# Norms applied after the products: weighted residual rows into TensorE, the factor per token into the results

## The chip, the cores and the metric

One NeuronCore of a Trainium2 chip runs the whole program in one launch. The metric is the device time of that execution in microseconds (us); lower is better.

## The reference, cut to what matters

Four decoder layers (mixers a, b, c, a) over 512 prompt tokens and 8 x 8 sample tokens, so 576 tokens of 1024 features, all in float32:

```
x = x + mixer(rmsnorm(x, g_mix));  x = x + convffn(rmsnorm(x, g_ffn))          per layer
rmsnorm(x, g) = x * rsqrt(mean(x*x, over features) + 1e-6) * g
conv_ffn:  u = xn @ w_up;  gate, val = u[:, :2816], u[:, 2816:]
           h = silu(causal_conv3(gate) + conv_b) * val;  return h @ w_down
fox (b):   proj = xn @ w_in  ->  q, k (normed per head of 64), v, g (sigmoid), logf
conv_mix (c): proj = xn @ w_in -> gb, gc, h;  z = causal_conv3(gc * h);  return (gb * z) @ w_out
```

There are eight norms: one ahead of each mixer and one ahead of each conv_ffn. The mixer of layers 0 and 3 (RWKV-7, "a") needs the normed rows themselves, to mix neighbouring tokens; the six other norms feed only matrix products, in which the factor per token, rsqrt(...), can be taken out of the product.

## The kernel before, in words

Activations lie with the features on the partitions: `x` is 8 rows of 128 features by 576 tokens. The weights come from HBM as 415 chunks of 1024 x 128 (512 KB), one after the other through four buffers `raw`. Each chunk is split on the fly into two float32r parts, `wh` on ScalarE (`split_hi`, L358) and `wl` on VectorE (`split_lo`, L365), each with two buffers; the activations are split in the same way into `xh`, `xl` (or `hh`, `hl`). A product is then hi*hi + hi*lo + lo*hi: `chunk_mm` (L368 to L386) runs 8 rows x 2 halves of 288 tokens x 3 matmuls = 48 matmuls for one chunk, into one of two PSUM tiles that alternate. The buffer of a chunk's weights comes free when the chunk is done (`s_mm`), a PSUM tile when its result has been read (`s_ev`). ScalarE, VectorE and TensorE each run their instructions in the order written; semaphores join them. Most phases are hardware loops (`Fori`), those of mixer a and the last down product are written out straight.

Each layer is a chain of phases: the mixer's products, the mixer proper, `out` (8 chunks, `res_*` with one chunk per tile), `up` (44 chunks, gate and value tiles in turn, `up_*`), `down` (24 chunks of 8, 8 and 6 rows, three per tile, `res_*`). In `res_*`, for each finished tile: ScalarE and VectorE first split the weights of the chunk that comes two later, then VectorE adds the tile to the row of `x` (L461), ScalarE squares the new row (L450), and TensorE, one tile later, sums the squares over the features with a matmul against ones (L478; the last row's at L425 in `add_squares`).

Behind the last row of squares stands the norm: ScalarE takes the root (`norm_act`, L410), VectorE the reciprocal (L391), and then for each of the 8 rows VectorE writes `xt` = x * g * rstd (L401), ScalarE copies it to `xh` (L413), and VectorE writes `xl` = xt - xh (L395). The first chunk of the next phase waits for `xl` row by row (`row_ready`, L376).

In `up_*`, ScalarE copies the gate tile out of PSUM (L507, L508) and makes the first tap of the convolution with its bias (L510); VectorE adds two taps (L527, L531); ScalarE applies silu (L514); VectorE multiplies with the value tile in PSUM (L536, L537) and the result is split into `hh` (ScalarE, L517) and `hl` (VectorE, L541). In layer 1, `qk_*` runs the 16 chunks of q and k first (per chunk: copy out of PSUM L1392, square L1397, a head sum on TensorE L1430, root L1384, reciprocal L1411, multiply L1414), in loops of four, with the head sum of each chunk behind the next chunk and the fourth head sum at the end of the iteration (L1439); then come the 16 chunks of v and g, with one copy or sigmoid each (L1368), and one chunk for the forget gate (`forget_*`, L1447 and on), behind which the attention starts.

Of the kernel before, what the change touches and what calls it, by code (L numbers as in the profile page):

```python
# [21 lines left out]
D = 1024  # L22
# [92 lines left out]
def build_program(nc, I, O, mixers=MIXERS):  # L115
# [3 lines left out]
    with ctx:  # L119
# [36 lines left out]
        cs = at("cs", [KF, 2 * NS], F32, f.take(4 * KF * 2 * NS))  # L156
        assert f.at <= nc.sbuf_usable_end, (f.at, nc.sbuf_usable_end)
# [13 lines left out]
        qn, rn = at("qn", [2, T], F32, b.at), at("rn", [2, T], F32, b.at + 8 * T)  # L171
        sc = at("sc", [2, 2, TP], F32, b.take(16 * TP))
# [73 lines left out]
        s_const, s_xin = sem("s_const"), sem("s_xin")  # L246
# [6 lines left out]
        s_sq, s_squ = sem("s_sq"), sem("s_squ")  # L253
        s_pad, s_t0, s_cv1, s_cv = sem("s_pad"), sem("s_t0"), sem("s_cv1"), sem("s_cv")
# [28 lines left out]
        NCONST = 2  # L283
        for layer, (kind, idx) in enumerate(mixers):
            names = []
            if kind == "a":
                names += [("r", 8, 8), ("k", 8, 8), ("v", 8, 8), ("g1", 1, 1), ("w1", 1, 1), ("a1", 1, 1)]
            elif kind == "b":
                names += [("qk", 16, 16), ("vg", 16, 16), ("f", 1, 1)]
            elif kind == "c":  # L290
                names += [("in", 24, 24)]
# [15 lines left out]
        n_norm, row0 = {}, {}  # L307
        q = r0 = 0
        for layer, (kind, _) in enumerate(mixers):
            if kind != "n":  # L310
                n_norm[layer, "mix"], row0[layer, "mix"] = q, r0
                q, r0 = q + 1, r0 + (len(MIX) if kind == "a" else 1) * KD
            n_norm[layer, "ffn"], row0[layer, "ffn"] = q, r0
            q, r0 = q + 1, r0 + KD
# [4 lines left out]
        def squ0(r):  # L319
            return KD + r * (2 + KD)  # L320

# [46 lines left out]
        def chunk_mm(pe, c, n, rh, rl, k0=0, nk=CH, first=True, last=True, i=0, cstep=0, nstep=0, row_ready=None,  # L368
                     row_used=None):
# [4 lines left out]
            for k in range(nk):  # L374
                if row_ready is not None:
# [13 lines left out]
        def norm_dve(dve, q, r0, col):  # L389
            dve.wait_ge(s_rs, q + 1)  # L390
            dve.reciprocal(rstd[:], rstd[:]).then_inc(s_rr, 1)  # L391

            def lo(k):
                dve.wait_ge(s_xh, r0 + k + 1)
                dve.tensor_tensor(xl[:, k], xt[:, k % 2], xh[:, k].bitcast(F32), ALU.subtract).then_inc(s_xl, 1)  # L395

            dve.wait_ge(s_rr, q + 1)
            for k in range(KD):
                if k >= 2:
                    dve.wait_ge(s_xl, r0 + k - 1)  # L400
                dve.scalar_tensor_tensor(xt[:, k % 2], x[:, k], par[:, col + k:col + k + 1], rstd[:],  # L401
                                         ALU.mult, ALU.mult).then_inc(s_xt, 1)
                if k >= 1:
                    lo(k - 1)
            lo(KD - 1)

        def norm_act(act, q, r0):
            act.activation(warm[:], eps[:], ACT.Sqrt)
            act.wait_ge(s_squ, KD + q * (2 + KD))
            act.activation(rstd[:], pst(STAT), ACT.Sqrt, bias=eps[:], scale=1.0 / D).then_inc(s_rs, 1)  # L410
# [18 lines left out]
        def rounds(eng, n, ph):  # L429

            if ph.c0 + ph.nch == NCHUNK:
# [7 lines left out]
        def res_act(act, ph, per):  # L439
# [3 lines left out]
            for i in rounds(act, 2, ph):  # L443
                for j in range(4):
                    for e in range(per):
                        split_hi(act, ph.c0 + per * j + e + 2, i, 4 * per)
                    n = ph.n0 + j
# [3 lines left out]
                        .then_inc(s_sq, 1)  # L451

        def res_dve(dve, ph, per):
            for i in rounds(dve, 2, ph):
                for j in range(4):
                    for e in range(per):
                        split_lo(dve, ph.c0 + per * j + e + 2, i, 4 * per)
# [1832 lines left out]
```

## Time and profile before

| | |
|---|---|
| median of 3 runs | 4210.56 us (4200.27 to 4211.14) |
| the profiled execution | 4210.09 us, span of its trace 4208.2 us |
| TensorE busy | 3826.8 us, 91% of the span |
| VectorE, ScalarE, GpSimd busy | 1793.6, 1512.9, 287.1 us |
| mean granted TensorE clock | 0.944 of full speed |
| read from HBM | 297.30 MB |

Busy time is the sum of an engine's instructions; the span runs from the first to the last instruction. TensorE's clock has two levels here, 2.4 GHz (1.00) and 1.2 GHz (0.50); a mean between them says what share of a stretch ran at which.

### The profile page before, as it was taken

Reading aid. Unit: us, or ns where it says so; the run is one execution under the profiler, and the core shown is the slowest. Engines: PE = TensorE matmul, PEld = TensorE weight load, DVE = VectorE, ACT = ScalarE, POOL = GpSimd, SP = SyncE. Lnnn points to the kernel's source line nnn. Section 1 sums busy time; section 2 is a strip of 40 time slices with the busy share of each in tenths; the row PEclk is TensorE's granted clock in tenths of the full one; section 3 lists DMA queues with packets and bytes.
Section 4 is the critical chain, followed back from the end, with each engine's and each line's share of the span. In section 5 each row is a group of like instructions: output and inputs, shape, how many; then the busy total and the mean of one; then the engine's idle time right before and its main releaser. Section 6 shows DMA issues by size and latency. Waiting matters only on the chain.

```text
span 4208.2 us, 93473 instructions
## 1 busy us (share of the span) xinstructions
PE 3826.8 (91%) x40189; PEld 3504.9 (83%) x40189; DVE 1793.6 (43%) x2245; ACT 1512.9 (36%) x2377; POOL 287.1 (7%) x556
## 2 busy tenths in 40 slices
PE   6968889899998989889998989999796888989999
PEld 5947784799998965589998989999794778489999
DVE  4375543444326434344423334432536554334432
ACT  2344441244323333334422224442233544124431
POOL 0011211000000000000000000000001212000000
PEclk9979996899999999999999999999897999689999
DMA  3200000122221258622222222222220000012222
GB/s 115 76 26 3 3 23 23 47 80 85 82 85 55 75 201 310 226 67 80 84 83 71 85 73 74 81 82 85 74 81 21 3 3 23 23 52 80 84 82 78
DMA packets 95902, 314.16 MB, mean 75 GB/s; under 512 B 18946, under 2 KB 20226, under 8 KB 94866
## 3 DMA queue, kind: packets, MB, share of 16 engines
q1 hardware_dynamic: 87410, 285.25, 20.6%
q10 hardware_dynamic: 8224, 24.88, 1.5%
q8 instruction: 223, 3.65, 0.4%
q14 instruction: 45, 0.37, 0.0%
HBM read 297.30 MB, written 12.79 MB: 74 GB/s over the span
## 4 chain that ended last, share of the span: by engine, by line
PE 56%; DVE 6%; ACT 4%; issue 1%; DMA 0%; ACTq 0%; SPq 0%; DVEq 0%
PE ps L381 14%; PE ps L383 14%; PE ps L382 14%; PE ps L993 3%; PE ps L478 1%; DVE xt L686 1%; PE ps L1237 1%; DVE xl L680 1%; DVE xt L401 1%; PE ps L1569 1%; PE ps L1230 1%; PE ps L1604 1%; PE ps L1624 1%; PE ps L1668 1%; PE ps L802 0%
## 5 line engine op out<-in xcount | busy, mean ns | idle before, releaser
L381 PE MATMUL ps<-xh,wh 128*128 128x288 f32 x4976 | 1504.3, 302 | 122.8 <-DVE xl L680 70.2
L382 PE MATMUL ps<-xl,wh 128*128 128x288 f32 x4976 | 1479.0, 297 | 0.0
L383 PE MATMUL ps<-xh,wl 128*128 128x288 f32 x4976 | 1473.0, 296 | 0.0
L365 DVE TENSOR_TENSOR wl<-raw,wh 128x1024 fp32r<-128x1024 f32 x415 | 508.3, 1225 | 1413.2 <-ACT wh L358 1412.9
L381 PEld LDWEIGHTS ps<-xh,wh 128*128 128x128 f32 x4976 | 943.0, 190 | 149.3 <-issue 97.1
L358 ACT ACTIVATE wh<-raw 128x1024 fp32r<-128x1024 f32 x415 | 440.0, 1061 | 1424.7 <-PE ps L383 1416.8
L382 PEld LDWEIGHTS ps<-xl,wh 128*128 128x128 f32 x4976 | 945.9, 190 | 2.3
L383 PEld LDWEIGHTS ps<-xh,wl 128*128 128x128 f32 x4976 | 947.4, 190 | 0.0
L381 PE MATMUL ps<-hh,wh 128*128 128x288 f32 x1536 | 463.4, 302 | 0.0
L383 PE MATMUL ps<-hh,wl 128*128 128x288 f32 x1536 | 455.4, 297 | 0.0
L382 PE MATMUL ps<-hl,wh 128*128 128x288 f32 x1536 | 448.6, 292 | 0.0
L382 PEld LDWEIGHTS ps<-hl,wh 128*128 128x128 f32 x1536 | 293.2, 191 | 2.1
L381 PEld LDWEIGHTS ps<-hh,wh 128*128 128x128 f32 x1536 | 289.2, 188 | 2.7 <-issue 0.6
L383 PEld LDWEIGHTS ps<-hh,wl 128*128 128x128 f32 x1536 | 288.4, 188 | 0.0
L993 PE MATMUL ps<-m,m 64*64 64x64 f32 x5952 | 228.5, 222 | 27.3 <-DVE m L1022 26.2
L993 PEld LDWEIGHTS ps<-m,m 64*64 64x64 f32 x5952 | 207.1, 139 | 32.2 <-DVE m L1022 28.2
L1022 DVE TENSOR_TENSOR m<-ps,m 128x512 f32<-128x512 f32 x100 | 68.7, 687 | 165.7 <-PE ps L993 165.6
L564 POOL COPY co<-gate 128x2 f32 x96 | 50.1, 522 | 1142.2 <-ACT gate L508 1014.2
L536 DVE TENSOR_TENSOR hf<-conv,ps 128x512 f32<-128x512 f32 x88 | 60.6, 688 | 155.1 <-PE ps L383 155.1
L701 ACT ACTIVATE xh<-xt 128x576 fp32r<-128x576 f32 x96 | 66.0, 687 | 106.8 <-DVE xt L686 106.2
L514 ACT ACTIVATE conv<-conv 128x592 f32<-128x592 f32 x88 | 61.6, 700 | 118.3 <-DVE conv L531 118.3
L1007 ACT ACTIVATE m<-ps 128x512 f32<-128x512 f32 x120 | 71.1, 595 | 81.1 <-PE ps L993 81.1
(300 smaller groups left out, 4565.7 us busy)
## 6 DMA issues: line engine op xcount, KB each, us to landing
raw<-in_w SPq DMA_DIRECT2D x415, 512.0 KB, 3.5
kp<-in_cache_k SPq DMA_DIRECT2D x64, 512.0 KB, 5.6
vp<-in_cache_v SPq DMA_DIRECT2D x64, 512.0 KB, 5.7
rkv<-in_wkv ACTq DMA_DIRECT2D x2, 2048.0 KB, 10.1
out_wkvs<-rkv ACTq DMA_DIRECT2D x2, 2048.0 KB, 7.3
x<-in_x ACTq DMA_DIRECT2D x1, 2304.0 KB, 13.0
out_k<-qk ACTq DMA_DIRECT2D x1, 2304.0 KB, 8.2
out_v<-vg ACTq DMA_DIRECT2D x1, 2304.0 KB, 13.0
```

The lines of the kernel that those rows point to most:

```text
L358: act.activation(wh[:, c % SPL], raw[:, c % RAWS], ACT.Copy).then_inc(s_hi, 1)
L365: dve.tensor_tensor(wl[:, c % SPL], raw[:, c % RAWS], wh[:, c % SPL].bitcast(F32), ALU.subtract).then_inc(s_lo, 1)
L381: pe.matmul(out, w_h, rhs_h, start=(first and k == 0), stop=False)
L382: pe.matmul(out, w_h, rhs_l, start=False, stop=False)
L383: mm = pe.matmul(out, w_l, rhs_h, start=False, stop=(last and k == nk - 1))
L514: act.activation(conv[:, u, 2:GW], conv[:, u, 2:GW], ACT.Silu).then_inc(s_si, 1)
L536: dve.tensor_tensor(tok(hf[:], 0), hist(conv[:, u], 0), tok(pst((n + 1) % 2), 0), ALU.mult)
L564: pool.tensor_copy(co[:, bass.ds(i * 2 + u, 1), 0:2], one(gate[:, u, GS - 2:GS]))
L701: act.activation(xh[:, k], xt[:, k % 2], ACT.Copy).then_inc(s_xh, 1)
L993: mm = pe.matmul(bank(bk)[r, p * CT:(p + 1) * CT], operand(sl, left, p)[r], mview("ist")[r] if right == "ist" else operand(sl, right, p)[r ...
L1007: act.activation(flat(sl[to][:]), bank(bk), ACT.Copy).then_inc(a_e, 1)
L1022: dve.tensor_tensor(sl[to][:], src, sl[by][:], ALU.add).then_inc(a_d, 1)
```

## The change

Six norms (all but the mixer norms of layers 0 and 3) are no longer applied to the rows that enter the products. `xh`, `xl` become the split of x * g, made row by row as soon as a row of `x` is final (`raw_hi`, `raw_lo`). Where the product that ends the row does not read `xh` (`down`, and `out` of layer 2) this stands inside the loop over the tiles; where it does (`out` of layers 0, 1 and 3) rows 0 to 6 are rewritten in place during the last tile, each when TensorE has used it (`s_gu`), and these phases are written out straight. The last sum of squares moves into the middle of the next phase's first chunk. The factor rstd is multiplied into the results on VectorE: into the gate tile as it leaves PSUM and into the activated gate in `up`; squared (`rs2`) and plain in the convolution mixer; into each tile in layer 1. ScalarE's copies out of PSUM go. In `res_*` the split of the weights for two chunks later stands behind the add and the square. In layer 1 the chunks of q/k and v/g alternate, written out straight, with the head sum behind each pair. The start waits for the constants, the parameters and x together.

```diff
@@ chunk_mm
             for k in range(nk):
+                if between is not None and k == nk // 2:
+                    between()
                 if row_ready is not None:
...
-        def norm_dve(dve, q, r0, col):
+        def norm_dve(dve, q, to):
             dve.wait_ge(s_rs, q + 1)
-            dve.reciprocal(rstd[:], rstd[:]).then_inc(s_rr, 1)
...
+            dve.reciprocal(to[:], to[:]).then_inc(s_rr, 1)
             dve.wait_ge(s_rr, q + 1)
-            for k in range(KD):
...
-                dve.scalar_tensor_tensor(xt[:, k % 2], x[:, k], par[:, col + k:col + k + 1], rstd[:],
-                                         ALU.mult, ALU.mult).then_inc(s_xt, 1)
...
-            for k in range(KD):
-                act.wait_ge(s_xt, r0 + k + 1)
-                act.activation(xh[:, k], xt[:, k % 2], ACT.Copy).then_inc(s_xh, 1)
+            act.activation(to[:], pst(STAT), ACT.Sqrt, bias=eps[:], scale=1.0 / D).then_inc(s_rs, 1)
+
+        def raw_hi(act, g, k, i=0):
...
+            act.activation(xh[:, bass.ds(i * 4 + k, 1)], x[:, bass.ds(i * 4 + k, 1)], ACT.Copy,
+                           scale=par[:, bass.ds(i * 4 + gain + k, 1)]).then_inc(s_gh, 1)
+
+        def raw_lo(dve, g, k, i=0):
...
+            dve.wait_ge(s_gh, i * 4 + KD * e + k + 1)
...
+            dve.scalar_tensor_tensor(xl[:, bass.ds(i * 4 + k, 1)], x[:, bass.ds(i * 4 + k, 1)],
+                                     par[:, bass.ds(i * 4 + gain + k, 1)],
+                                     xh[:, bass.ds(i * 4 + k, 1)].bitcast(F32), ALU.mult, ALU.subtract)\
+                .then_inc(s_gl, 1)
+
+        def by_norm(dve, out, src, r):
+            for part in range(2):
+                op = dve.tensor_tensor(out(part), src(part), tok(r, part), ALU.mult)
+            return op
@@ res_act (res_dve likewise: raw_lo for raw_hi, the add for the square)
-            for i in rounds(act, 2, ph):
+            for i in rounds(act, 2, ph, place is not None):
                 for j in range(4):
-                    for e in range(per):
+                    for e in range(per - 1):
                         split_hi(act, ph.c0 + per * j + e + 2, i, 4 * per)
+                    if place is not None and i * 4 + j == KD - 1:
+                        for k in range(KD - 1):
+                            act.wait_ge(s_gu, place * (KD - 1) + k + 1)
+                            raw_hi(act, g, k)
...
                         .then_inc(s_sq, 1)
+                    if g is not None and (place is None or i * 4 + j == KD - 1):
+                        raw_hi(act, g, j, i)
+                    split_hi(act, ph.c0 + per * j + per + 1, i, 4 * per)
@@ res_pe, rows_pe
-            add_squares(pe, 1, sq0(r) + 1 + KD, stop=True)
+            if g is None:
+                last_squares(pe, r)
+
+        def first_chunk(pe, c, n, q, e):
+            chunk_mm(pe, c, n, xh, xl, row_ready=(s_gl, KD * e + 1), between=lambda: last_squares(pe, q - 1))
...
+            for c in range(per):
+                if c == 0:
+                    first_chunk(pe, ph.c0, ph.n0, q, e)
+                else:
+                    chunk_mm(pe, ph.c0 + c, ph.n0 + c, xh, xl)
+            with pe.Fori(0, ph.nch // per - 1) as i:
+                for c in range(per, 2 * per):
+                    chunk_mm(pe, ph.c0 + c, ph.n0 + c, xh, xl, i=i, cstep=per, nstep=per)
@@ up_act
-                    act.wait_ge(s_mm, i * 4 + c + 1)
-                    act.wait_ge(s_pad, i * 2 + p + 1)
-                    act.activation(gate[:, u, 2:GS], tok(pst(n % 2), 0), ACT.Copy)
-                    act.activation(hist(gate[:, u], 1), tok(pst(n % 2), 1), ACT.Copy).then_inc(s_ev[n % 2], 1)
@@ up_dve
+                    dve.wait_ge(s_mm, i * 4 + c + 1)
+                    dve.wait_ge(s_pad, i * 2 + p + 1)
+                    by_norm(dve, lambda part: hist(gate[:, u], part), lambda part: tok(pst(n % 2), part), rstd[:])\
+                        .then_inc(s_ev[n % 2], 1)
                     split_lo(dve, c + 2, i, 4)
...
+                    dve.wait_ge(s_si, i * 2 + layer * KF + u + 1)
+                    by_norm(dve, lambda part: hist(conv[:, u], part), lambda part: hist(conv[:, u], part), rstd[:])\
+                        .then_inc(s_sr, 1)
                     dve.wait_ge(s_mm, i * 4 + c + 2)
@@ convmix_dve (ScalarE's copy of the first tile goes)
+                    dve.wait_ge(s_mm, i * 12 + c + 1)
+                    dve.tensor_tensor(sq[:, u], pst(n % 2), rs2[:], ALU.mult).then_inc(s_ev[n % 2], 1)
...
+                    by_norm(dve, lambda part: hist(conv[:, u], part), lambda part: hist(conv[:, u], part), rstd[:])\
+                        .then_inc(s_sr, 1)
@@ layer 1: qk_*, store_act, plain_dve give way to
+        def proj_act(act, layer):
+            for u in range(NQ):
+                c, n = ph.c0 + 2 * u, ph.n0 + 2 * u
+                split_hi(act, c + 2)
+                act.wait_ge(s_ev[n % 2], turns(n) + 1)
+                act.activation(qn[:, u % 2], qk[:, u], ACT.Square).then_inc(b_hsq, 1)
+                split_hi(act, c + 3)
+                act.wait_ge(b_hsm, u + 1)
+                if u >= 2:
+                    act.wait_ge(b_hn, u - 1)
+                act.activation(rn[:, u % 2], pst(3), ACT.Sqrt, bias=eps[:], scale=1.0 / 64).then_inc(b_hrt, 1)
+                if u >= KD:
+                    act.wait_ge(s_ev[(n + 1) % 2], turns(n + 1) + 1)
+                    act.activation(vg[:, u], vg[:, u], ACT.Sigmoid)
...
+            for u in range(NQ):                                  # proj_dve
+                dve.wait_ge(s_mm, c + 1)
+                dve.tensor_tensor(qk[:, u], pst(n % 2), rstdb[:], ALU.mult).then_inc(s_ev[n % 2], 1)
+                split_lo(dve, c + 2)
+                if u:
+                    head_norm(u - 1)                             # reciprocal, then multiply
+                dve.wait_ge(s_mm, c + 2)
+                dve.tensor_tensor(vg[:, u], pst((n + 1) % 2), rstdb[:], ALU.mult).then_inc(s_ev[(n + 1) % 2], 1)
+                split_lo(dve, c + 3)
+            head_norm(NQ - 1)
...
+                chunk_mm(pe, c + 1, n + 1, xh, xl)               # proj_pe
+                pe.wait_ge(b_hsq, u + 1)
+                if u:
+                    pe.wait_ge(b_hrt, u)
@@ forget_dve
+            dve.wait_ge(s_mm, ph.c0 + 1)
+            dve.tensor_tensor(lf[0:16], pst(ph.n0 % 2)[0:16], rstdb[0:16], ALU.mult).then_inc(s_ev[ph.n0 % 2], 1)
```

## Rows read from the trace of the kernel before

**Rows 1.** The page: TensorE's busy row, its clock in 40 slices, the chain by engine.

```profile
PE 3826.8 (91%) x40189; PEld 3504.9 (83%) x40189; DVE 1793.6 (43%) x2245; ACT 1512.9 (36%) x2377; POOL 287.1 (7%) x556
...
PEclk9979996899999999999999999999897999689999
...
PE 56%; DVE 6%; ACT 4%; issue 1%; DMA 0%; ACTq 0%; SPq 0%; DVEq 0%
```

**Rows 2.** Windows round norms: start:end length, busy (instructions) by engine, clock, DMA.

```profile
1831.40:1855.65 24.25, 12.80 (x58) 10.31 (x57) 17.62 (x19) 10.75 (x15) 0.31 (x2) 0.72 0.10 29
...
2280.90:2304.19 23.29, 11.30 (x58) 9.19 (x57) 17.63 (x19) 9.34 (x13) 0.30 (x2) 0.78 0.10 34
...
sum 142.81, PE 73.77 PEld 59.83 DVE 105.77 ACT 57.59 POOL 1.50; mean PE 12.29 PEld 9.97 DVE 17.63 ACT 9.60 POOL 0.25
```

**Rows 3.** Timeline, third norm: start, length, engine, line, [idle before <- ended by].

```profile
1831.20 1.13 PE L478 MATMUL ps<-sq,con 128*128 128x288 f32 x4
...
1831.40 1.06 ACT L358 ACTIVATE wh<-raw 128x1024 fp32r<-128x1024 f32 x1 [3.39 <-PE ps L383]
...
1832.49 1.22 DVE L365 TENSOR_TENSOR wl<-raw,wh 128x1024 fp32r<-128x1024 f32 x1 [5.47 <-ACT wh L358]
...
1833.63 0.75 DVE L461 TENSOR_TENSOR x<-x,ps 128x576 f32 x1
...
1834.59 0.68 ACT L450 ACTIVATE sq<-x 128x576 f32 x1 [2.13 <-DVE x L461]
...
1835.32 2.27 PE L425 MATMUL ps<-sq,con 128*128 128x288 f32 x4 [2.99 <-ACT sq L450]
...
1837.64 0.74 ACT L410 ACTIVATE rstd<-ps,eps 128x576 f32<-128x576 f32 x1 [0.85 <-PE ps L425]
...
1838.41 3.75 DVE L391 RECIPROCAL rstd<-rstd 128x576 f32<-128x576 f32 x1 [4.03 <-ACT rstd L410]
...
1842.20 1.55 DVE L401 SCALAR_TENSOR_TENSOR xt<-x,par,rstd 128x576 f32<-128x576 f32 x2
...
1844.67 0.58 PE L381 MATMUL ps<-xh,wh 128*128 128x288 f32 x1 [7.07 <-DVE xl L395]
...
1850.66 0.40 PE L381 MATMUL ps<-xh,wh 128*128 128x288 f32 x1 [0.46 <-DVE xl L395]
```

**Rows 4.** Windows without a norm (columns of rows 2): unrolled, out, up.

```profile
58.24:96.64 38.40, 38.40 (x290) 38.40 (x289) 7.36 (x6) 9.59 (x13) 0.00 (x0) 1.00 0.25 83
...
1824.04:1831.40 7.36, 7.36 (x53) 7.16 (x52) 1.89 (x2) 1.74 (x2) 0.00 (x0) 1.00 0.25 71
...
1855.65:2130.84 275.19, 275.15 (x2064) 274.92 (x2062) 120.69 (x150) 132.76 (x173) 17.55 (x86) 1.00 0.26 82
```

**Rows 5.** Windows, one per iteration of the q/k loop (columns of rows 2).

```profile
1318.84:1352.32 33.48, 31.24 (x210) 29.93 (x209) 23.07 (x12) 11.76 (x17) 0.00 (x0) 0.95 0.19 63
...
1385.73:1417.63 31.90, 29.66 (x210) 28.50 (x209) 21.72 (x12) 11.76 (x16) 0.00 (x0) 1.00 0.24 69
...
sum 132.32, PE 123.37 PEld 118.21 DVE 90.92 ACT 47.04 POOL 0.00; mean PE 30.84 PEld 29.55 DVE 22.73 ACT 11.76 POOL 0.00
```

**Rows 6.** Timeline: end of a q/k iteration; start of a down phase.

```profile
1343.12 1.55 PE L1430 MATMUL ps<-qn,con 128*128 128x288 f32 x4 [2.24 <-ACT rn L1384]
...
2133.11 1.24 PE L425 MATMUL ps<-sq,con 128*128 128x288 f32 x4 [2.31 <-ACT sq L442]
```

**Rows 7.** Groups of the up phase, 1858 to 2130: busy us, mean ns, idle before.

```profile
L527 DVE SCALAR_TENSOR_TENSOR conv<-gate,par,conv 128x592 f32<-128x592 f32 x22 | 18.4, 835 | 12.1 <-ACT conv L510 12.1
...
L536 DVE TENSOR_TENSOR hf<-conv,ps 128x512 f32<-128x512 f32 x21 | 14.4, 687 | 36.0 <-PE ps L383 36.0
...
L537 DVE TENSOR_TENSOR hf<-conv,ps 128x64 f32<-128x64 f32 x21 | 4.5, 215 | 0.0
...
L514 ACT ACT_TABLE_LOAD x11 | 14.1, 1283 | 0.2
```

**Rows 8.** Timeline: first step behind the forget gate's chunk.

```profile
1521.06 0.71 ACT L1447 ACTIVATE lf<-ps,par 16x576 f32<-16x576 f32 x1
```

More of the change, by code:

```diff
@@ L320, in squ0, with norm_behind @@
             return KD + r * (2 + KD)
+        def norm_behind(layer, name):
+            nxt = (layer, "ffn") if name == "out" else (layer + 1, "mix")
+            if nxt not in raw_norm:
+                return None
+            return PC["gm" if nxt[1] == "mix" else "gf", nxt[0]], raw_norm[nxt]
         def turns(n):
@@ L435, in rounds, with res_act @@
                     yield i
-        def res_act(act, ph, per):
+        def res_act(act, ph, per, g=None, place=None):
             r = ph.res
@@ L462, in res_dve, with last_squares, res_pe @@
                         .then_inc(s_ev[n % 2], 1)
-        def res_pe(pe, ph, per, rh, rl, ready, row_ready=None):
+                    if g is not None and (place is None or i * 4 + j == KD - 1):
+                        raw_lo(dve, g, j, i)
+                    split_lo(dve, ph.c0 + per * j + per + 1, i, 4 * per)
+        def last_squares(pe, r):
+            add_squares(pe, 1, sq0(r) + 1 + KD, stop=True)
+        def res_pe(pe, ph, per, rh, rl, ready, row_ready=None, g=None, place=None):
             r = ph.res
@@ L1403, in qk_dve @@
-        def qk_dve(dve, layer):
-            ph = plan[layer, "qk"]
-            for half in range(2):
-                g = qg8[:] if half == 0 else par[:, PC["kg", 0]:PC["kg", 0] + 1]
-                with dve.Fori(0, 2) as i:
-                    def norm(j):
-                        r = 8 * half + j
-                        dve.wait_ge(b_hrt, i * 4 + r + 2)
-                        dve.reciprocal(rn[:, j % 2], rn[:, j % 2]).then_inc(b_hrc, 1)
-                        dve.wait_ge(b_hrc, i * 4 + r + 1)
-                        row = qk[:, bass.ds(i * 4 + r, 1)]
-                        dve.scalar_tensor_tensor(row, row, g, one(rn[:, j % 2]), ALU.mult, ALU.mult)\
-                            .then_inc(b_hn, 1)
-                    for j in range(4):
-                        split_lo(dve, ph.c0 + 8 * half + j + 2, i, 4)
-                        if j:
-                            norm(j - 1)
-                    norm(3)
@@ L1423, in qk_pe @@
[L1423 to L1439 removed]
+        NQ = 2 * KD
@@ L1532, in fox_sp @@
         def fox_sp(sp, layer, done):
-            first, last = plan[layer, "vg"].c0, plan[layer, "out"].c0 + SPL + RAWS
+            first, last = plan[layer, "qkvg"].c0 + 2 * KD, plan[layer, "out"].c0 + SPL + RAWS
             weights_in(sp, done, first + RAWS)
-            sp.wait_ge(s_mm, plan[layer, "qk"].c0 + 1)
+            sp.wait_ge(s_mm, plan[layer, "qkvg"].c0 + 1)
             sp.dma_start(pgs[0:1], I["pages"]).then_inc(b_pg, 16)
```

240 lines of the change are left out of this document (110 added, 130 removed).

## The prediction

> **What bounds the kernel now.** I read the page's busy rows and chain first. TensorE is busy 91% of the span, no other engine half of it, and the chain that ended last runs mostly over TensorE; the clock stands near full speed but dips at single slices [rows 1]. So what counts is where TensorE waits or runs slowly. Next I cut the trace into phases. Inside `up` TensorE is never idle: 43 chunks take 275.19 us, 6.40 each, at clock 1.00, in a loop of eleven iterations; the straight code of mixer a keeps the same 6.40 (six chunks in 38.40); a tile of `out` takes 7.36, so the four square-sum matmuls cost 0.96 [rows 4]. DMA brings 512 KB per chunk at a quarter of its capacity [rows 4], so it is not near a limit. The time that TensorE loses lies at the norms and in layer 1's q/k loop.
>
> A norm, seen in the timeline [rows 3]: the last chunk ends just ahead of 1831.40. Then, in series: the weight splits for a later chunk (ScalarE 1.06, VectorE 1.22), the add 0.75, the square 0.68, the last square-sum (TensorE had been idle 2.99), root 0.74, reciprocal 3.75, then row by row. TensorE starts at 1844.67 after 7.07 us idle, and even then is fed slower than it works: VectorE hands over a row each 1.52 us (two operations of 0.76, half of the 1.55 for two), where TensorE uses one in 0.80; the 0.46 idle at the row of 1850.66 repeats at each later row. Measured from the chunk end before the norm to the end of the first chunk behind it, the six norms of the change take 142.81 us, 24.25 the longest kind and 23.29 the shortest kind shown, at a mean clock of 0.72 to 0.78 [rows 2]: after the pause the first matmuls ran at the 1.2 GHz level.
>
> **The change, part by part.**
>
> *Norm gaps.* After the change nothing between the last chunk and the next one needs rstd. What TensorE must still do in that stretch: the square-sum of the last but one row (0.96), the chunk (6.40), the last square-sum (0.96, now in the middle of the chunk): 8.3 us. Six times 8.3 is 49.8; 142.8 - 49.8 = 93.0 us saved, if all covers hold. They are, with t = 0 at the end of the last chunk:
>
> Where the rows are made inside the loop (three norms): add 0.1 to 0.9, square to 1.7, x * g to 2.4, its split to 3.3, the weight split by ScalarE to 3.5 and VectorE to 4.7. TensorE reaches the last square-sum at 0.96 + 3.2 = 4.2 and row 7 at 0.96 + 5.6 + 0.96 = 7.5. Nothing is late; the spare is 2.5 us at the square.
>
> In place (`out` of layers 0, 1, 3): ScalarE first has the weight split of the tile before (to 2.7 after that chunk's end), then seven copies of about 0.71, so until 7.7, 0.3 behind the chunk's end at 7.36. VectorE starts its seven at 4.0 at 0.78 each (L401's pace) and ends at 9.5, t = 2.1. Add to 2.9, square to 3.7: TensorE wants it at 4.2. Row 7 is ready at 5.2, wanted at 7.5. The weights of the second chunk are split at 6.8, wanted at 8.3. This is the thinnest cover, 0.5 us; if gone it costs what it is late by, three times.
>
> Then rstd: square-sum done at 5.3; ScalarE must load a table (1.28 [rows 7]) and take the root, so up to t = 7.7 in place; the reciprocal ends at 11.5; the gate tile is multiplied until 12.4; then VectorE splits the weights of the third chunk, to 13.7. TensorE starts that chunk at 8.3 + 6.4 = 14.7. Spare 1.0 us in place, about 2.6 elsewhere. So the stall is not moved there.
>
> *Inside `up`.* ScalarE loses a copy (two pieces) per pair of chunks, VectorE gains two multiplications in two pieces. For each I take the row of the nearest kind, 0.687 + 0.215 = 0.90 [rows 7], so 1.8 us per pair of 12.8. VectorE had per pair two weight splits (2.45), two taps (1.67), the product (0.90) and hl (0.75): 5.8, now 7.6 of 12.8. In order, t = 0 at the gate chunk's end: gate to 1.0; weight split behind it to 2.3; taps 2.4 to 4.1; silu to 4.9; second multiplication to 5.8; the value tile is ready at 6.4, as before; product to 7.4; next weight split to 8.8, wanted at 12.8. All waits that VectorE gains have the weight split queued behind them, and that has 4 us to spare. Cost on the path: 0. Bounds for one new multiplication: below, 0.75 (an unsplit one, L461 [rows 3]); above, for want of a nearer limit, the slowest VectorE operation over 576 columns, 3.75 [rows 3]. I take 0.90, the row with the same two pieces.
>
> *Convolution mixer.* Per three chunks (19.2 us) VectorE gains 0.75 + 0.90 and stands at about 10: 0.
>
> *Layer 1.* The q/k loop takes 132.32 us for 16 chunks and 16 head sums; 16 * 6.40 + 16 * 0.96 would be 117.8. The excess is at the end of each iteration, where the fourth head sum follows the third at once and waits 2.24 us for ScalarE's root [rows 6], and where the clock then falls (0.95 over such an iteration, 1.00 over the last one) [rows 5]. In the new order a head sum follows the v/g chunk, 6.4 us behind the q/k chunk whose square it needs (ready at 1.9), and the root before it is 6 us old. So 14.5 us go. VectorE per pair of 13.8 us: 0.75 + 1.22 + 3.75 + 0.82 + 0.75 + 1.22 = 8.5; the v/g tile is ready at 6.4, when the reciprocal and multiply of the pair before (2.3 to 6.9) are nearly through; the next split ends at 8.9, wanted at 13. 0.
>
> From pair 8 on ScalarE alternates root and sigmoid, 16 table loads at 1.28 [rows 7] where there were about two. Per pair: 2.1 + 0.7 + 0.7 + 0.7 + 2.6 = 6.8 of 13.8; the sigmoid ends at 11.6. Cost 0 but for the tail: the last head norm now runs until 14.3, behind the forget chunk's end at 13.8, so VectorE's new multiplication of that tile ends at 15.1, and ScalarE's first step, which came 1.1 us behind the chunk [rows 8], comes at about 1.4: +0.3 us, on the path, since TensorE idles there.
> The Trainium skill, "ScalarE: Activation LUTs", section "What ACT_TABLE_LOAD costs", adds a drain to each switch, 2.66 us together, and its rule is to batch by table set, which speaks against this order. By that figure (an estimate) a pair would hold ScalarE 9.6 us, still covered, and the tail would be some 1.4 us worse. The trace shows the 1.283 alone.
>
> *Order in `res`.* The add now comes ahead of the splits. Inside a phase nothing waits for it. At the norm of layer 3's mixer, which stays and looks like rows 3, 2.2 us of splits leave the path to the square-sum, and ScalarE's split then precedes its table load, giving 0.3 back: 1.9 saved.
>
> *Straight code and peeled iterations.* The first 2, 4 or 12 chunks of a phase now stand ahead of the loop. Loop ends inside `up`, and straight code, both show 6.40 per chunk [rows 4]. But each hand-over from a loop to the next phase lay under a wait until now, such as 2.31 us in front of `down` [rows 6]. So it costs 0 to 2.3 us each. I take 0, by the loop ends that show none.
>
> **Sum.** The profiled execution took 4210.1 (span 4208.2, 1.9 around it), 0.5 under the median of the runs. 4210.1 - 93.0 - 14.5 - 1.9 + 0.3 = 4101.0. Forecast 4101 us, 2.6% less. TensorE's idle time and its slow stretches go together; the matmuls stay the same in number.
>
> **Rivals.**
>
> *A. Hand-overs show.* With no wait over them, leaving a loop or entering the next one stalls TensorE's instruction stream. For: no row shows such a hand-over uncovered. Against: loop ends show nothing. Twelve places (an exit and an entry per norm) at half to all of 1.2 to 2.3 us give 10 to 28 us: 4111 to 4129, say 4117.
> The Trainium skill, "Runtime: NRT & Kernel Launch", section "Instruction fetch mechanics", says that a taken branch to code outside the fetched window stalls. [...]
>
> *B. The stall moves to the third chunk.* If ScalarE or VectorE runs 3 us later than my schedule in place, rstd comes late, VectorE holds back the gate tile and the weights behind it, and TensorE waits before chunk three, then starts at the low clock. Against: 1.0 us of spare in place, more elsewhere. Price 3 to 5 us at each of six: 4119 to 4131.
>
> *C. VectorE becomes the bound in `up`: slower than before.* 88 pairs. It decides when the new operations lift VectorE's ring (5.8 + two multiplications) over 12.8 us, so above 3.5 each; the price is then the excess, 88 times. With 3.75 each the ring is 13.3 and the time 4145; to lose more than the 109 gained it takes 1.24 us per pair, a ring of 14.1, 4.1 per multiplication, or long waits for the silu in series with them. Then 4215 to 4250. For: every PSUM tile's release now hangs on VectorE. Against: its idle share, and rows that cost 0.9.
>
> *D. The change does not do what it says*: PE stays idle as now because the first chunk still waits for something behind the norm. Only the q/k loop gains: 4195. The diff shows no such wait.
>
> **Chances.** Forecast (4093 to 4110) 0.64; A 0.18; B 0.06; C 0.04 (half of it slower than before); D 0.02; faster than 4093, by something that I charged too high, 0.06. The range 4092 to 4120 holds the forecast, most of A and the start of B, so a little over 8 in 10. A measurement of this kernel can tell about 0.3%, 13 us, from no change: faster than that 0.95, within it 0.02, slower 0.03.
>
> **What would show it.** In the profile after: chunk ends before and behind each of the six norms 8.3 us apart, at clock 1.00; no idle time of TensorE with L381 behind `xl` there; the q/k and v/g chunks in pairs of 13.8 us; pairs of `up` still 12.8; VectorE's busy time up by some 160 us in `up`, ScalarE's down by 70; mean clock near 0.96. Wrong would be: stalls of 1 to 3 us at the first or third chunk (A or B), `up` pairs over 12.8 (C), TensorE waiting for the square at the middle of the first chunk in place.

## The result, and the profile after

The changed kernel takes 4095.49 us (median of 4 runs, 4089.57 to 4097.33), the kernel before 4207.67 beside it: ratio 0.973, interval 0.9716 to 0.9744. The forecast was 4101 us, 2.6% less; measured are 5.5 us less than that, and 2.7%. The profiled execution took 4089.57 us, its span is 4087.7.

The page of the changed kernel, the rows that answer to [rows 1] (busy TensorE, its clock, the chain):

```profile
PE 3781.7 (93%) x40189; PEld 3475.4 (85%) x40189; DVE 1935.2 (47%) x2605; ACT 1445.9 (35%) x2180; POOL 402.8 (10%) x556
...
PEclk8989997899999999999999999999898999699999
...
PE 83%; DVE 9%; ACT 6%; issue 1%; DMA 0%; ACTq 0%; SPq 0%; DVEq 0%
```
TensorE is busy 93% of the span instead of 91%, with 3781.7 us instead of 3826.8 for the same 40189 instructions (fewer of them at the low clock). The chain's 56% and 83% can't be compared as they stand: in the kernel before it could be followed back only to 1401 us, 67% of the span, in the changed kernel over 99%, and TensorE has 84% of what was followed in both. The clock's slices of 102 us are too coarse to show a norm: but for the first one (the start of the program, 0.92 before and 0.90 after) their low places lie in mixer a and stay. The mean clock rose from 0.944 to 0.957.

Windows, cut alike in both traces: from the start of the square-sum behind the last tile of one phase to the next phase's first square-sum (in layer 1 to the first matmul behind the forget chain). Each line: start:end length, then busy us of TensorE, its weight loads, VectorE, ScalarE, GpSimd, the clock, DMA. The kernel before, the first two stretches and the sum of all six:

```profile
810.35:1111.99 301.64, 288.09 (x2122) 285.44 (x2120) 140.25 (x173) 144.21 (x189) 17.88 (x88) 0.98 0.24 77
...
1261.01:1528.55 267.54, 238.64 (x1658) 230.77 (x1656) 133.71 (x88) 93.76 (x120) 2.27 (x5) 0.95 0.26 82
...
sum 1646.82, PE 1548.50 PEld 1527.93 DVE 772.72 ACT 727.61 POOL 91.19; mean PE 258.08 PEld 254.65 DVE 128.79 ACT 121.27 POOL 15.20
```
The changed kernel:

```profile
801.80:1087.80 286.00, 283.70 (x2122) 283.04 (x2120) 165.11 (x249) 126.55 (x139) 46.61 (x88) 1.00 0.25 82
...
1235.39:1472.67 237.28, 228.54 (x1658) 224.52 (x1657) 144.95 (x106) 89.78 (x100) 2.26 (x5) 0.99 0.29 93
...
sum 1539.53, PE 1519.00 PEld 1511.69 DVE 883.59 ACT 638.69 POOL 206.80; mean PE 253.17 PEld 251.95 DVE 147.27 ACT 106.45 POOL 34.47
```
A norm with its `up` phase goes from 301.64 to 286.00 us, at clock 1.00; layer 1's projections from 267.54 to 237.28; the six together from 1646.8 to 1539.5, 107.3 less. VectorE gains (140 to 165 us in the first line), ScalarE loses (144 to 127).

The stretch of a norm alone in the changed kernel, the third one, from the square-sum behind the last tile to the end of the first chunk (the same columns):

```profile
1778.10:1786.43 8.33, 8.33 (x58) 7.91 (x57) 5.87 (x7) 5.87 (x8) 0.86 (x2) 1.00 0.24 72
```
All six take 8.32 to 8.34 us there, with no idle time of TensorE, where the kernel before takes the 23.2 to 24.3 of [rows 2].

The timeline of the norm of [rows 3] in the changed kernel (start, length, engine, line, what was idle before):

```profile
1778.10 1.13 PE L524 MATMUL ps<-sq,con 128*128 128x288 f32 x4
...
1778.86 0.51 PE L401 MATMUL ps<-xh,wh 128*128 128x288 f32 x1
...
1779.64 0.74 DVE L500 TENSOR_TENSOR x<-x,ps 128x576 f32<-128x576 f32 x1
...
1780.42 0.69 ACT L483 ACTIVATE sq<-x 128x576 f32<-128x576 f32 x1 [2.14 <-DVE x L500]
...
1782.27 1.13 PE L454 MATMUL ps<-sq,con 128*128 128x288 f32 x4
...
1784.14 0.72 ACT L417 ACTIVATE rstd<-ps,eps 128x576 f32<-128x576 f32 x1
...
1784.89 3.75 DVE L411 RECIPROCAL rstd<-rstd 128x576 f32<-128x576 f32 x1 [0.92 <-ACT rstd L417]
...
1788.97 0.82 DVE L441 TENSOR_TENSOR gate<-ps,rstd 128x512 f32<-128x512 f32 x2 [0.32 <-DVE rstd L411]
...
1789.70 1.22 DVE L383 TENSOR_TENSOR wl<-raw,wh 128x1024 fp32r<-128x1024 f32 x1
```
TensorE goes from the square-sum (L524) to the next phase's first chunk (L401) at once. Add, square, root and reciprocal still stand one behind the other, but beside the chunk; the first gate tile is multiplied at 1788.97, and the split for the third chunk ends at 1790.9, when TensorE is still in the second.

Groups of VectorE in a part of layer 1's `up` (1815 to 2060 us), changed kernel (busy us, mean ns | idle before):

```profile
L441 DVE TENSOR_TENSOR gate<-ps,rstd 128x512 f32<-128x512 f32 x19 | 13.1, 692 | 66.6 <-PE ps L403 66.6
...
L441 DVE TENSOR_TENSOR gate<-ps,rstd 128x64 f32<-128x64 f32 x19 | 4.1, 215 | 0.0
...
L589 DVE TENSOR_TENSOR hf<-conv,ps 128x512 f32<-128x512 f32 x19 | 13.1, 689 | 14.4 <-PE ps L403 14.4
```

### The profile page after: what moved, and what is told of

The parts are those of the page before. It is cut to its first block, busy times and chain, and to the rows that moved or that the text cites. A ratio compares the mean times of both kernels' runs of the same rounds, so it can differ in the third digit from the quotient of the medians.

```text
span 4087.7 us, 93200 instructions
## 1 busy us (share of the span) xinstructions
PE 3781.7 (93%) x40189; PEld 3475.4 (85%) x40189; DVE 1935.2 (47%) x2605; ACT 1445.9 (35%) x2180; POOL 402.8 (10%) x556
## 4 chain that ended last, share of the span: by engine, by line
PE 83%; DVE 9%; ACT 6%; issue 1%; DMA 0%; ACTq 0%; SPq 0%; DVEq 0%
PE ps L401 21%; PE ps L403 20%; PE ps L402 20%; PE ps L1053 6%; DVE xt L746 2%; PE ps L1297 2%; PE ps L524 1%; DVE xl L740 1%; PE ps L1290 1%; PE ps L862 1%; PE ps L1327 1%; DVE a_zz L912 1%; PE ps L454 1%; PE ps L1610 1%; PE ps L875 1%
## 5 line engine op out<-in xcount | busy, mean ns | idle before, releaser
L401 PE MATMUL ps<-xh,wh 128*128 128x288 f32 x4976 | 1495.7, 301 | 74.8 <-DVE xl L740 73.3
L401 PEld LDWEIGHTS ps<-xh,wh 128*128 128x128 f32 x4976 | 936.2, 188 | 93.3 <-issue 51.2
L401 PE MATMUL ps<-hh,wh 128*128 128x288 f32 x1536 | 463.1, 302 | 0.0
L401 PEld LDWEIGHTS ps<-hh,wh 128*128 128x128 f32 x1536 | 289.2, 188 | 2.6 <-issue 0.7
L617 POOL COPY co<-gate 128x2 f32 x96 | 113.8, 1185 | 1045.8 <-DVE gate L441 914.8
L441 DVE TENSOR_TENSOR gate<-ps,rstd 128x512 f32<-128x512 f32 (+1 forms) x176 | 72.4, 453 | 293.2 <-PE ps L403 291.9
L483 ACT ACTIVATE sq<-x 128x576 f32<-128x576 f32 (+1 forms) x64 | 44.0, 687 | 343.4 <-DVE x L500 183.1
L500 DVE TENSOR_TENSOR x<-x,ps 128x576 f32<-128x576 f32 (+1 forms) x64 | 48.2, 754 | 209.4 <-PE ps L403 209.4
L441 DVE TENSOR_TENSOR conv<-conv,rstd 128x512 f32<-128x512 f32 x192 | 79.5, 456 | 67.7 <-ACT conv L560 67.5
```

The source lines that it names most:

```text
L401: pe.matmul(out, w_h, rhs_h, start=(first and k == 0), stop=False)
L441: op = dve.tensor_tensor(out(part), src(part), tok(r, part), ALU.mult)
L500: dve.tensor_tensor(row, row, pst(n % 2).rearrange("p (o t) -> p o t", o=1), ALU.add)\
L617: pool.tensor_copy(co[:, bass.ds(i * 2 + u, 1), 0:2], one(gate[:, u, GS - 2:GS]))
```

## The experiments

"Before" stands in them for the kernel before, "changed" for the kernel with the change. "In place" are the norms behind `out` of layers 0, 1 and 3 (the first, third and sixth); at the other three the rows are made in the loop. Each ratio is to runs of before made beside the kernel (medians 4208.84 in experiments 1 to 3, 4211.66 in 4 to 6 and for one reciprocal in 7, 4208.08 for two and in 9, one run of 4214.63 in 8). A difference "over changed" is taken from the 4096.97 us of experiment 1, so from experiment 4 on it compares runs made beside different series; the ratios give 60.6, 16.4 and 6.3 us for the 63.7, 19.2 and 6.9 below, and each has an interval of some 7 us to either side. What the stretches of the traces show is finer than that.

### 1. Both kernels once more

> The kernel before, unchanged, once more with a profile. In the first two profiles the work of mixer a in layer 0 (from the last of its weight chunks, at 249 us, to the first tile of out) took 8.6 us less in the changed kernel, though no line of it was changed. Theory 1 (it varies from execution to execution, by where the clock falls): this stretch, and the same one in layer 3, comes out several us away from the first profile of the same kernel, while each of the six norm stretches stays within 1 us of 24.0. Rival (something in the change speeds mixer a up): the stretch repeats the first profile within 1 us.

> The changed kernel, unchanged, once more. Theory 1 (norm gaps 93, q/k loop 14.5, order at layer 3's mixer 2, tail 0.3): the parts that the change touches repeat their sum of 109 us less within 1 us, and the rest of the difference of the profiled executions (11 us) moves. Rival (mixer a is faster by the change): its two stretches are again 8.6 and 4.0 us shorter than in the kernel before. Ratio to before 0.972 to 0.975.

Before: 4211.6 us in one run; changed: 4096.97 (4 runs), ratio 0.9733 (0.9716 to 0.9749). Windows from mixer a's last projection chunk to the first tile of `out`, layer 0, in the order before, before again, changed, changed again:

```profile
249.19:758.78 509.59, 430.88 (x8825) 339.06 (x8825) 244.70 (x290) 181.62 (x394) 96.81 (x78) 0.85 0.04 13
```
```profile
249.19:756.84 507.65, 429.70 (x8824) 339.20 (x8825) 244.45 (x289) 181.03 (x394) 96.45 (x77) 0.86 0.04 13
```
```profile
248.83:750.24 501.41, 422.30 (x8825) 332.89 (x8826) 244.70 (x290) 181.61 (x394) 96.82 (x78) 0.87 0.04 13
```
```profile
248.83:752.10 503.27, 424.10 (x8830) 333.88 (x8829) 245.41 (x290) 181.88 (x395) 96.84 (x78) 0.86 0.04 13
```
So the stretch repeats within 2 us, and taken alone that would have spoken for the rival, as would layer 3's: 732.6 us in both profiles of before, 728.5 and 728.2 in those of changed. But the kernels below have the same mixer a too, and from about 249 us they reach the first tile at 755.9 and 756.0 (two built from before), and at 759.0, 759.1, 750.1, 756.3, 758.7, 758.5 and 752.3 (seven built from changed). Layer 3's takes 732.5 to 732.7 in the four traces of before's kind and 726.6 to 734.3 in the nine of changed's. Both ranges of changed's kind hold before's values: the first profile of the changed kernel fell on a short one. The parts that the change touches do not vary: 286.00 us in both profiles of changed. Theory 1 holds for the size of the 8.2 and 4.1 us; whether a small part of them belongs to the change is open, for the means over these traces are 1.4 us (layer 0) and 1.9 us (layer 3) lower in changed's kind.

### 2. The head sums alone

Before, with the loop of four (L1425 to L1439) written out straight in all three engines:

```diff
-            with pe.Fori(0, 4) as i:
-                for j in range(4):
-                    chunk_mm(... j ...)
-                    if j:
-                        heads_sum(j - 1)
-                heads_sum(3)
+            for r in range(2 * KD):
+                chunk_mm(... r ...)
+                if r:
+                    heads_sum(r - 1)
+            heads_sum(2 * KD - 1)
```

> The kernel before with one part of the change's effect alone: the sixteen q/k chunks written out straight, with each head sum behind the next chunk, also across what were the ends of the loop's iterations; no pairs with v/g, norms as before. Theory 1 (the excess of 14.5 us in the q/k loop is the fourth head sum that follows the third at once, and the low clock behind it): three of the four double head sums go, so 3/4 of the iterations' excess: three iterations at 4.1 us, about 12 us less, 0.997 of before; the double one at the very end stays (2.5 us). Rival (the excess is VectorE's reciprocals, 4.6 us per chunk with a split of 1.2 behind, so that only pairing with v/g helps): under 3 us less.

4198.34 us, 10.5 less than the 4208.84 beside it, ratio 0.9973 (0.9961 to 0.9985). From the first head sum to the last it took 107.2 us, where before took 119.3 and 118.2 in its two profiles: the 12 us expected. Layer 1, from the last tile before it to its `out`, went from 509.57 to 497.89. Waits of TensorE in the q/k stretch (total us, times, longest): one is left, the one at the end:

```profile
PE ps L1419 <- ACT rn L1382: 2.3, 1, 2.3
```
### 3. The order of split and add alone

Before, with the last `split_hi` / `split_lo` of each tile moved behind the square / the add in `res_act`, `res_dve`.

> The kernel before with another part alone: in the out and down phases the weight split for two chunks later stands behind the add and the square. Theory 1: at all seven norms that follow such a phase 2.2 us of splits leave the path to the square-sum; ScalarE's split then stands ahead of its table load and gives 0.3 back: about 13 us less, 0.997 of before. Rival (the splits are wanted early, for the next phase's second chunk, and come late): 0 to 5 us less at the norms. In the changed kernel the same edit can be worth this only at layer 3's mixer (2 us).

4192.91 us, ratio 0.996 (0.9945 to 0.9974). The last norm with its `up` (301.72 in before):

```profile
3736.19:4035.05 298.86, 287.12 (x2123) 284.91 (x2121) 140.38 (x173) 146.25 (x189) 18.45 (x88) 0.98 0.24 78
```
2.9, 2.1, 1.2, 2.1 and 2.9 us less at the five norms outside layer 1, 2.0 at that one, 2.1 at layer 3's mixer: 15.2 of the 15.9 us by which the median is lower, a little more than was expected. The change contains this part: some 13 us of the 93 of the prediction.

### 4. TensorE made to wait for rstd again

```diff
-            chunk_mm(pe, c, n, xh, xl, row_ready=(s_gl, KD * e + 1), between=lambda: last_squares(pe, q - 1))
+            last_squares(pe, q - 1)
+            pe.wait_ge(s_rr, q + 1)
+            chunk_mm(pe, c, n, xh, xl, row_ready=(s_gl, KD * e + 1))
```

> The changed kernel, but at the six norms the last square-sum stands ahead of the first chunk and TensorE then waits until the reciprocal is done; rows, tiles and all else as changed. It splits the norm gap's 93 us in two: what the wait for rstd costs, and what the feeding row by row cost. Theory 1: TensorE has its 0.96 us, waits for the square (0 to 1.9), 1 us of sum, table load and root 0.7 to 2.5, reciprocal 3.75; the chunk starts at about t = 9 to 11 instead of 1, and its first part runs at the low clock (1.5 to 2 us): 9 to 11 us per norm, 55 to 65 in all, so about 4155; the other 30 us of the 93 were the feeding. Rival (the feeding was the larger part): under 45 us more.

4160.7 us, 63.7 over changed, as theory 1 had it. TensorE's rows at the third norm, behind layer 1's `out` (length, idle before), and the window that answers to the 286.00:

```profile
1810.01 1.24 PE L454 MATMUL ps<-sq,con 128*128 128x288 f32 x4 [1.92 <-ACT sq L483]
...
1817.56 0.61 PE L401 MATMUL ps<-xh,wh 128*128 128x288 f32 x1 [6.31 <-DVE rstd L411]
```
```profile
1806.96:2103.68 296.72, 286.19 (x2122) 284.83 (x2120) 165.16 (x249) 127.77 (x140) 47.59 (x88) 0.98 0.24 79
```
The five norms outside layer 1 take 10.0, 10.7, 9.9, 8.1 and 10.1 us more, 48.8 together. With experiment 3 this cuts the 77.0 us that these five gained in three: 48.8 for not waiting for rstd, 11.1 for the order, and the rest, 17.1, for what lies between the kernel of experiment 3 and this one. By the rows that is above all that the rows are ready, where they were handed over one each 1.52 us; no run takes this last part alone.

### 5. The last square-sum ahead of the first chunk

As experiment 4, without the line that waits for `s_rr`.

> The changed kernel with the last square-sum ahead of the first chunk instead of in its middle, with no wait for the reciprocal. Theory 1: TensorE now stands until the square is there: t = 1.7 to 1.9 where rows are made in the loop (0.9 us of waiting), and 3.0 in place, so about 0.8 us at three norms and 2 us at three: 8 us, a little more if the clock falls at one of them: 0.002 above the changed kernel. Rival (the middle place is worth nothing, the square is early enough): under 2 us.

4116.2 us, 19.2 over changed, more than twice what was expected. At an in-place norm:

```profile
813.71 1.24 PE L454 MATMUL ps<-sq,con 128*128 128x288 f32 x4 [1.93 <-ACT sq L483]
...
815.24 0.44 PE L401 MATMUL ps<-xh,wh 128*128 128x288 f32 x1
...
817.40 0.44 PE L401 MATMUL ps<-xh,wh 128*128 128x288 f32 x1
```
The wait is the one worked out (1.93 us), but behind it, at two of the three in-place norms, the first matmuls run at the low clock, 0.44 us where they take 0.29: 3.7 us in all. At the third norm the wait is 1.92 us and the clock stays: 2.2. At those with rows made in the loop it is 1.2 (0.9 of waiting), 13 together. The rest is not at the norms: each of the four `down` phases took 149.1 instead of 147.6, for their matmuls too started at the low clock behind the 2.3 us of idle time, as they did in before at two of four, while `out` of layer 2 started at the high clock and took 1.5 us less than in changed: 4.6 net. The miss is the clock: 2 us of idle time brought it down at some places and not at others.

### 6. The old order in the changed kernel

The edit of experiment 3 undone.

> The changed kernel with the old order in the out and down phases: weight splits ahead of the add and the square. Theory 1: the square comes 2.2 us later, at t = 4 where rows are made in the loop (wanted at 4.2: just covered) and at 5.2 or later in place (wanted at 4.2): 1 to 2 us at each of three norms, 2 us at layer 3's mixer: 5 to 8 us more than the changed kernel. Rival (the order is free but for layer 3's mixer): 2 us. Other rival (the rows of x times g come too late for the first chunk): TensorE waits with L401 at row 7, over 10 us.

4103.85 us, 6.9 over changed; the intervals of the two ratios (0.9731 to 0.9764 here) overlap, so the traces must decide. TensorE waits for the last square, in the middle of the chunk, at the three in-place norms only, which lengthens each by 1.0 us (0.73 of it idle), and at layer 3's mixer the 2.1 us are lost again:

```profile
1786.99 1.24 PE L454 MATMUL ps<-sq,con 128*128 128x288 f32 x4 [0.73 <-ACT sq L484]
```
In place the square had 1.2 us to spare (below) and now comes 2.2 later: 1.0 is what is left over. Where rows are made in the loop the cover of 2.5 us just holds: these norms take at most 0.1 us more. That is 5.1 us, the lower end of what theory 1 gave. In the profiled execution three of the four `down` phases started at the low clock besides (149.1 us each, 4.6 together).

### 7. More work for VectorE

```diff
+                    for d in range(1):                       # second kernel: range(2)
+                        dve.wait_ge(s_dm, ...)
+                        dve.reciprocal(rs2[:], rstd[:]).then_inc(s_dm, 1)
```

at the end of each pair in `up_dve`; the result is read by nobody.

> The changed kernel with one more VectorE operation per pair of chunks in up, behind hl: a reciprocal of rstd into a spare row, 3.75 us, nobody reads it. VectorE then holds 7.6 + 3.75 = 11.4 us of each 12.8. Theory 1 (VectorE has room to 12.8 us per pair, its own work is what counts): 0 to 5 us more. Rival C in a milder form (long waits for the silu in series with VectorE's work make the ring longer than its work): the ring is over 12.8 and each pair is late by 0.5 to 1.5 us: 45 to 130 us more.

> The changed kernel with two reciprocals of rstd into a spare row per pair of chunks in up, 7.5 us more on VectorE, which nobody reads. VectorE's work per pair is then 15.1 us against TensorE's 12.8. Theory 1 (VectorE becomes the bound once its work passes 12.8): 2.3 us per pair for the work alone, up to 4 with the waits for silu in series; 88 pairs: 200 to 350 us more, slower than the kernel before. If it is under 100 us more, VectorE's durations are not what bounds its ring.

One reciprocal: 4094.53 us, the changed kernel's time. Two: 4335.23, 1.03 of before. The third norm with its `up`, one and two (columns as above, VectorE's busy time is the fourth number):

```profile
1783.74:2069.74 286.00, 283.69 (x2123) 283.04 (x2121) 238.82 (x270) 127.86 (x140) 46.31 (x88) 1.00 0.25 82
```
```profile
1844.12:2187.64 343.52, 302.17 (x2123) 296.91 (x2121) 316.06 (x291) 127.49 (x140) 40.21 (x88) 0.95 0.21 68
```
With VectorE busy 238.8 of 286.0 us nothing moves; at 15.1 us per pair of 12.8 it is the bound: 2.6 us per pair in the four `up` windows, 2.7 by the whole time. Rival C of the prediction sets in where the prediction put it, when VectorE's ring (all that it does for a pair, one piece behind the other) passes 12.8 us, and the change has at least 3.75 us per pair to spare.

### 8. GpSimd's copies, released later

```diff
                     pool.wait_ge(s_ev[n % 2], i * per + turns(n) + 1)
+                    pool.wait_ge(s_sr, i * 2 + r + 1)
```

> The changed kernel, but GpSimd's two copies of the convolution's last columns (128x2 and 128x16) wait for the second multiplication by rstd instead of only for the first. In the kernel before they took 0.46 and 0.19 us; in the changed kernel 1.20 and 0.82, and there each ends within 0.1 us of the VectorE instruction that runs beside it (1801.80 and 1801.76; 2.56 and 2.50). Theory 1 (GpSimd's copy does not finish before the VectorE instruction beside it does): released where VectorE then idles 0.76 us, the copies take about 0.4 and 0.2 again. Rival (their length comes from the tile being written by VectorE instead of ScalarE, or from the code around them): they stay near 1.2 and 0.8. The time stays that of the changed kernel, 4090 to 4100, in both.

4100.4 us in one run. The copies in `up` (busy, mean ns):

```profile
L618 POOL COPY co<-gate 128x2 f32 x19 | 3.5, 184 | 228.5 <-DVE conv L441 228.5
...
L619 POOL COPY co<-gate 128x16 f32 x19 | 3.7, 197 | 0.0
```
184 and 197 ns: theory 1, for the first copy even less than the 0.4 us expected. What it explains stands in the last section.

### 9. A version that beats both: no idle time at the start of `down`

```diff
-            add_squares(pe, 1, sq0(r) + 1, start=True)
-            if ready:
-                pe.wait_ge(*ready)
+            if place is None:
+                pe.wait_ge(s_rs, r + 1)
+                pe.wait_ge(s_z, r // 2 + 1)
+                for a in range(2):
+                    mm = pe.matmul(pst(STAT, a * HT, (a + 1) * HT), zero[:], con[:, 0:HT], start=True, stop=False)
+                mm.then_inc(s_squ, 1)
+            else:
+                add_squares(pe, 1, sq0(r) + 1, start=True)
...
+                        if ready and j == 0:
+                            pe.wait_ge(ready[0], ready[1] + k0 + nk)
```

with a tile `zero` that VectorE clears behind the norms ahead of `up` in layers 0, 1 and 3 and behind the one ahead of layer 2's mixer.

> The changed kernel with the idle time at the start of the four down phases and of layer 2's out taken away: TensorE clears the sum of squares with a matmul against a tile of zeros instead of waiting for ScalarE's zeroed row, and waits for the rows of the gated product eight at a time (in out row by row) instead of for the last one. Theory 1: TensorE's 2.3 us idle ahead of each of these five places (and 0.2 around it) goes, 12.5 us, and with it the low clock that follows the idle time in some executions (1.5 us at 0 to 5 places): 12 to 18 us less than the changed kernel, about 4082. Rival (another wait takes its place: the weights of the second chunk, or the first rows): TensorE idles at the same places elsewhere in the first or second chunk, under 4 us less in all.

4081.37 us (5 runs), ratio to before 0.9698 (0.9684 to 0.9711), 15.6 under the changed kernel (14.7 by the ratios). From the last tile of one phase to the first tile of the next the four stretches that end in `down` take 2.6, 2.7, 2.8 and 2.6 us less than in changed, and the one that ends in layer 2's `out` 4.2, because its first chunk no longer runs at the low clock. TensorE has no idle time in any of the five, so theory 1 holds and the wait did not move, and `down` runs at full speed throughout:

```profile
1087.39:1234.81 147.42, 147.42 (x1091) 145.74 (x1090) 41.29 (x41) 35.36 (x40) 0.00 (x0) 1.00 0.27 86
```
## Why the prediction was right, step by step

- **Norm gaps.** Forecast 93.0 us for six, of which 15.8 in layer 1: 77.2 for the other five; measured 77.0 (15.6, 15.9, 15.1, 14.7, 15.7). The 8.3 us between chunk ends followed from four matmuls, a chunk and four matmuls, and nothing else appeared between them: 8.32 to 8.34 us at all six.
- **In place.** Square ready at t = 3.7 by the schedule; measured from L524's start it was ready at 3.0 (1780.42 + 0.69 against 1778.10), so the spare was nearer 1.2 than 0.5, as VectorE's seven row operations ended at 1.6 and not 2.1. Experiment 6 shows that it is thin all the same.
- **The stall is not moved.** Reciprocal done at 10.5, gate tile at 11.7, split for chunk three at 12.8; wanted at 14.7. The prediction had the reciprocal at 11.5, so the spare was nearer 2 us than 1. Rival B did not come.
- **VectorE in `up`.** 0.692 + 0.215 us per multiplication against 0.90 taken; TensorE's 286.00 us have no idle time but the known 2.3 ahead of `down`. Experiment 7 shows the room: at least 3.75 us per pair, under 7.5. Of what the forecast said would show, 160 us more on VectorE in `up` are 160 piece by piece (176 multiplications of 0.907; the page's two L441 groups, 152 with the convolution mixer, count overlapping pieces once), and the copies that ScalarE lost were 70 in before (L507 and L508, 50.9 + 19.0).
- **Layer 1.** 30.3 us less in the window, forecast 15.8 + 14.5 - 0.3 = 30.0. Experiment 2 shows 11 to 12 of the 14.5 by the head sums alone. The tail was a little shorter than the 0.3 charged: TensorE sits idle 8.74 us behind the forget gate's chunk, where it sat 8.56.
- **Table loads.** Inside layer 1's pairs they cost nothing on the path. ScalarE's rows at the last head norm:

```profile
1459.04 0.74 ACT L1435 ACTIVATE rn<-ps,eps 128x576 f32<-128x576 f32 x1
...
1459.80 1.28 ACT L1438 ACT_TABLE_LOAD   x1
...
1461.10 0.69 ACT L1438 ACTIVATE vg<-vg 128x576 f32<-128x576 f32 x1
```
The load stands right behind the root and the sigmoid right behind the load, 1.28 us in between and no more. The estimate from the Trainium skill ("ScalarE: Activation LUTs", "What ACT_TABLE_LOAD costs") with a drain of 1.38 us on top is not what this trace shows; the measurement decides.

- **Order at layer 3's mixer.** 1.9 forecast, 2.1 measured.
- **Hand-overs.** Rival A did not come: TensorE has no idle time at the norms, in straight code, at loop ends or at loop entries. Where `up` hands over to `down`, the 2.3 us wait still lay over it in the changed kernel; experiment 9 takes it away, and no idle time shows there either. (The lower end of the rival's price was a slip: half of twelve places at 1.2 us is 7 us, not 10.)

The touched parts together: 107.3 + 2.1 = 109.4 us less, forecast 109.1. What the profiled execution had beyond that, 11.1 us, can be read off: mixer a took 8.2 and 4.1 us less (experiment 1), the attention 2.1 more (244.17 against 242.03), the starts of `out` and `down` 0.6 less and the start of the program 0.4 less. At the starts of phases the low clock fell on other places: two `down` phases won 1.4 and 1.5, and `out` of layer 2 lost 1.6, taking 9.02 us to its first tile instead of 7.43, a cost that the forecast did not have. That these nearly cancel was luck. The medians lie 112 us apart, 3 more than the sum. The starts of phases (0.6 us less in this pair of profiles, 2.6 in that of experiment 1) and mixer a's lower mean can make that up, but that they are the cause was not shown.

The prediction also says that the time that TensorE loses lies at the norms and in the q/k loop. More of it lies in mixer a, 79 us idle in layer 0's stretch and 115 in layer 3's (509.59 - 430.88, 732.60 - 617.87), which the change leaves alone. And the one thing that the forecast left unsaid is that a seventh of its 93 us came from an edit that needs none of the others.

## What to carry to other kernels

Here a factor per token, moved behind the product, cost TensorE nothing, because the engine that multiplies it in had room. Count that room per period against the engine that sets the time, and add work that nobody reads to see where it ends. Look at what stands ahead of the last result of a phase in program order: here work for a later chunk stood ahead of an add that everybody waited for, worth 15 us in the traces for a few moved lines. And compare stretches between the same two instructions, not whole executions: the untouched part of this program varies by more than some of the effects.

## What the runs showed of the hardware that was not expected

GpSimd's small copies became 2.6 and 4.1 times longer (means of 463 to 1187 ns and 192 to 789, layer 1) though nothing in them changed. Changed kernel, then before:

```profile
1800.53 1.23 DVE L383 TENSOR_TENSOR wl<-raw,wh 128x1024 fp32r<-128x1024 f32 x1 [0.18 <-ACT wh L376]
...
1800.59 1.21 POOL L617 COPY co<-gate 128x2 f32 x1 [9.31 <-DVE gate L441]
...
1801.67 0.83 DVE L577 SCALAR_TENSOR_TENSOR conv<-gate,par,conv 128x592 f32<-128x592 f32 x1
...
1801.74 0.82 POOL L618 COPY co<-gate 128x16 f32 x1
```
```profile
1869.54 1.23 DVE L365 TENSOR_TENSOR wl<-raw,wh 128x1024 fp32r<-128x1024 f32 x1 [4.50 <-ACT wh L358]
...
1870.34 0.47 POOL L564 COPY co<-gate 128x2 f32 x1 [12.02 <-ACT gate L508]
...
1870.75 0.19 POOL L565 COPY co<-gate 128x16 f32 x1
```
In both, a copy ends with the VectorE instruction that runs beside it (1801.80 with 1801.76, 1802.56 with 1802.50; 1870.81 with 1870.77), and before's second copy takes 0.19 us with none beside it. Experiment 8 moves both copies to where VectorE is idle and gets 0.18 and 0.20. The Trainium skill, "SBUF — State Buffer", section "SBUF: two separate sides", says that VectorE, when it reads two operands from SBUF, and GpSimd, when it reads SBUF too, hold a shared port in turn, each for a whole instruction. The trace agrees: beside both long copies of the changed kernel VectorE reads two tiles (`raw` and `wh`, `gate` and `conv`). It cost nothing here: `up` with its norm takes 286.00 us with the long copies and with experiment 8's short ones, for nobody waits for them.

After idle times of about 2 us TensorE's clock fell at some places and not at others of the same kernel (`down` in before: 149.0, 147.6, 147.5 and 149.0 us), and at one place in one execution and not in the next. The `down` phase of layer 1 in the two profiles of before:

```profile
2133.11:2280.70 147.59, 147.59 (x1088) 145.76 (x1089) 33.55 (x32) 29.21 (x30) 0.00 (x0) 1.00 0.27 84
```
```profile
2133.09:2282.18 149.09, 149.09 (x1089) 147.20 (x1090) 33.55 (x32) 29.21 (x30) 0.00 (x0) 0.99 0.26 84
```
So a short wait had two prices here, about 1.5 us apart; what decides between them no run shows.
